# Value weights multiplied in pairs: one 512-column product over two weight slots, keys and values in another order

## The reference, cut to what matters

```
def shared_kv(x, g, w_kv):
    kv = rmsnorm(x, g) @ w_kv
    k, v = jnp.split(kv, 2, axis=-1)
...
def memory_cross_attention(u, mem_n, w_q, w_kv, w_o):
    q = (u @ w_q).reshape(b, t, MEM_HEADS, MEM_HEADDIM)
    k, v = jnp.split(mem_n @ w_kv, 2, axis=-1)
    ...
    p = jax.nn.softmax(logits, axis=-1).astype(v.dtype)
    o = jnp.einsum('bhtm,bmhd->bthd', p, v).reshape(b, t, D_MODEL)
    return o @ w_o
```

## Time and profile before

| | |
|---|---|
| median of three runs | 933.07 us (932.87 to 933.37) |
| the profiled execution | 933.03 us, span 931.2 us |
| TensorE busy | 917.2 us, 98% of the span |
| VectorE busy | 620.1 us, 67% |
| ScalarE busy | 497.9 us, 53% |
| DMA | 163.31 MB, mean 175 GB/s |

### The profile page before, as it was taken

The page is one execution under the profiler, slowest core; times in us unless marked ns, Lnnn a source line. Parts: engine busy times, 40 slices in busy tenths (PEclk is TensorE's granted clock), DMA queues, the critical chain, the costliest instruction groups (busy, mean ns, idle before and its releaser), DMA issues.

```text
span 931.2 us, 14494 instructions
## 1 busy us (share of the span) xinstructions
PE 917.2 (98%) x5972; PEld 822.5 (88%) x5972; DVE 620.1 (67%) x750; ACT 497.9 (53%) x721; POOL 56.0 (6%) x68
## 2 busy tenths in 40 slices
PE   8999999999999999999999999999999899999997
PEld 7999998878899898888888999987998798888885
DVE  6888466895765687777744764775755748777543
ACT  6565467664654564444434753665744645444333
POOL 1000003460000000000000220000000000000000
PEclk9999999999999999999999999999999899999999
DMA  9865454225562475555555696433642455555551
GB/s 276 274 187 184 142 155 132 94 99 181 181 226 92 136 229 193 196 192 181 182 195 203 212 285 214 136 137 120 215 164 91 157 172 189 182 180 183 200 204 45
DMA packets 121210, 163.31 MB, mean 175 GB/s; under 512 B 4093, under 2 KB 106933, under 8 KB 121158
## 3 DMA queue, kind: packets, MB, share of 16 engines
q1 hardware_dynamic: 117830, 151.47, 49.9%
q0 software_dynamic: 3328, 11.10, 3.8%
HBM read 161.49 MB, written 1.07 MB: 175 GB/s over the span
## 4 chain that ended last, share of the span: by engine, by line
PE 94%; DVE 3%; ACT 2%; issue 1%; DVEq 0%; ACTq 0%
PE bank L465 25%; PE bank L533 16%; PE bank L548 9%; PE bank L476 8%; PE bank L481 8%; PE bank L487 8%; PE bank L539 8%; PE bank L647 2%; PE bank L853 1%; PE bank L824 1%; PE bank L742 1%; PE bank L959 1%; PE bank L659 0%; PE bank L949 0%; DVE w_lo L1336 0%
## 5 line engine op out<-in xcount | busy, mean ns | idle before, releaser
L1336 DVE TENSOR_TENSOR w_lo<-w_raw,w_hi 128x2048 fp32r<-128x2048 f32 x135 | 308.8, 2292 | 134.9 <-ACT w_hi L991 134.4
L991 ACT ACTIVATE w_hi<-w_raw 128x2048 fp32r<-128x2048 f32 x135 | 257.4, 1913 | 201.3 <-DMA w_raw<-in_ffn_w_gu_dram 96.3
L533 PE MATMUL bank<-actT,w_hi 128*128 128x512 f32 x640 | 152.9, 391 | 0.1
L533 PEld LDWEIGHTS bank<-actT,w_hi 128*128 128x128 f32 x640 | 117.6, 188 | 23.1 <-issue 0.2
L539 PEld LDWEIGHTS bank<-actT,w_lo 128*128 128x128 f32 x640 | 82.0, 191 | 3.1
L539 PE MATMUL bank<-actT,w_lo 128*128 128x256 f32 x640 | 83.0, 283 | 0.0
L476 PE MATMUL bank<-actT,w_hi 128*128 128x256 f32 x560 | 74.3, 285 | 0.0
L481 PE MATMUL bank<-actT,w_hi 128*128 128x256 f32 x560 | 72.9, 283 | 0.0
L487 PE MATMUL bank<-actT,w_lo 128*128 128x256 f32 x560 | 72.9, 283 | 0.0
L476 PEld LDWEIGHTS bank<-actT,w_hi 128*128 128x128 f32 x560 | 69.6, 191 | 1.3 <-issue 0.8
L481 PEld LDWEIGHTS bank<-actT,w_hi 128*128 128x128 f32 x560 | 69.7, 192 | 0.0
(11 more groups left out here) (239 smaller groups left out, 1354.4 us busy)
## 6 DMA issues: line engine op xcount, KB each, us to landing
w_raw<-in_ffn_w_gu_dram SPq DMA_DIRECT2D x44, 1024.0 KB, 5.1
w_raw<-in_ffn_w_down_dram SPq DMA_DIRECT2D x22, 1024.0 KB, 4.9
w_raw<-in_ssm_w_in_dram SPq DMA_DIRECT2D x20, 1024.0 KB, 5.4
w_raw<-in_mem_w_kv_dram SPq DMA_DIRECT2D x16, 1024.0 KB, 5.5
w_raw<-in_ssm_w_out_dram SPq DMA_DIRECT2D x8, 1024.0 KB, 5.0
w_raw<-in_mem_w_q_dram SPq DMA_DIRECT2D x8, 1024.0 KB, 6.4
w_raw<-in_mem_w_o_dram SPq DMA_DIRECT2D x8, 1024.0 KB, 5.0
w_raw<-in_w_kv_dram SPq DMA_DIRECT2D x8, 1024.0 KB, 5.5
```

The lines of the kernel that those rows point to most:

```text
L533: pe.matmul(bank[:, b + c, :], hi[:, slot, cols], actT[:, k].rearrange("p e n -> p (e n)"), start=k == 0, stop=False, skip_group_check=True)
L991: act.activation(hi[:, u % SLOTS, :], raw[:, u % SLOTS, :], ACT.Copy).then_inc(w_hi_done, 1)
L1336: dve.tensor_tensor(lo[:, s, :], raw[:, s, :], hi[:, s, :].bitcast(F32), ALU.subtract).then_inc(w_lo_done, 1)
```

## The change

`MOBA_UNITS` is put into the order mk0, mk1, mv0, mv1, mk2, mk3, mv2, mv3. Eight V units (`v0` 2 and 3, `v1` 2 and 3, all of `mv`) are multiplied in pairs by a new function `wide`: one matmul has the stationary token tile as before, but streams 512 columns, 256 out of the slot of the first unit and 256 out of that of the second. Where the first unit of a pair stood, TensorE now makes token tile 0 for both units, where the second stood, tile 1 for both; each bank holds one token tile and is copied out in one piece. The first of the two waits for `w_hi` and `w_lo` of both units. Both slots are released together, after tile 1 (`w_used` by 2); the copy of tile 0 waits for a new semaphore, `wide_mm`. A half for `turn` is now four of the eight blocks of input channels. The outputs of head pairs 0 to 3 need both units of the first `mv` pair, those of 4 to 7 both of the second.

```diff
@@ -58,7 +58,8 @@
 C_ID, C_TRI, C_CAUS, C_HOT, C_END = 0, P, P + S, 2 * P + S, 2 * P + 2 * S
 
 
-MOBA_UNITS = [(name, i) for i in range(D // TC) for name in ("mk", "mv")]
+MOBA_UNITS = [(name, i + k) for i in range(0, D // TC, 2) for name in ("mk", "mv") for k in range(2)]
+WIDE = [("v0", 2), ("v0", 3), ("v1", 2), ("v1", 3), *[("mv", i) for i in range(D // TC)]]
 KIND = {"xbc": "T", "z": "T", "w_out": "M", "k0": "T", "v0": "V", "q0": "T", "wo0": "M", "gu0": "T", "down0": "M",
         "mq": "T", "mk": "T", "mv": "V", "mo": "M", "k1": "T", "v1": "V", "q1": "T", "wo1": "M", "gu1": "T", "down1": "M"}
 
@@ -103,6 +104,7 @@
 
 BANKED = [("params", 0)] + [n for n in NAME_OF if KIND[n[0]] != "M" and not (n[0] == "gu1" and n[1] < HEAD)]
 V_OF = {n: v for v, n in enumerate(BANKED)}
+WIDES = [n for n in BANKED if n in WIDE]
 FREED = []
 _n = {"act": 0, "dve": 0}
 for _name, _i in BANKED:
@@ -313,6 +315,7 @@
         head_turned, head_hi, head_lo = sem("head_turned"), sem("head_hi"), sem("head_lo")
         gate_ready, h_ready = sem("gate_ready"), sem("h_ready")
         stored = sem("stored")
+        wide_mm = sem("wide_mm")
 
         class Own:
 
@@ -557,8 +560,35 @@
                 pe.wait_ge(w_lo_done, u + 1)
                 return v_products(u % SLOTS, b, act_hi, lo, halves, last=True)
 
+            def wide(name, i, act_hi, act_lo, parts=range(2)):
+                t, u, v = i % 2, U[(name, i - i % 2)], V_OF[(name, i)]
+                s, s1 = u % SLOTS, (u + 1) % SLOTS
+                assert U[(name, i - t + 1)] == u + 1
+                for part in parts:
+                    if part == 0:
+                        e, n = FREED[v - 2]
+                        pe.wait_ge(t_out[e], n)
+                    for act, w in ((act_hi, hi), (act_lo, hi), (act_hi, lo)):
+                        if part == 0 and t == 0 and act is act_hi:
+                            pe.wait_ge(w_lo_done if w is lo else w_hi_done, u + 2)
+                        for k in range(part * KD // 2, (part + 1) * KD // 2):
+                            one = w[:, s, k * TC:(k + 1) * TC]
+                            both = bass.AP(one.tensor, one.offset, [list(one.ap[0]), [(s1 - s) * UNIT, 2], [1, TC]])
+                            ins = pe.matmul(bank[:, v % 2, :], act[:, k, t * P:(t + 1) * P], both,
+                                            start=act is act_hi and w is hi and k == 0, stop=w is lo and k == KD - 1,
+                                            skip_group_check=True)
+                    if part:
+                        if t:
+                            ins.then_inc(w_used, 2)
+                        else:
+                            ins.then_inc(wide_mm, 1)
+
             def banked(name, i, act_hi, act_lo, free=None):
 
+                if (name, i) in WIDE:
+                    wide(name, i, act_hi, act_lo)
+                    return
                 u, v = U[(name, i)], V_OF[(name, i)]
                 e, n = free or FREED[v - 2]
                 pe.wait_ge(t_out[e], n)
@@ -574,6 +604,9 @@
 
             def fill_half(name, i, half):
 
+                if (name, i) in WIDE:
+                    wide(name, i, memT_hi, memT_lo, [half])
+                    return
                 u, v = U[(name, i)], V_OF[(name, i)]
                 if half == 0:
                     e, n = FREED[v - 2]
@@ -961,7 +994,7 @@
                 if s > BLAG:
                     p = s - BLAG - 1
                     pe.wait_ge(b_probT, p + 1)
-                    e, n = FREED[V_OF[("mv", p // 2)]]
+                    e, n = FREED[V_OF[("mv", p // 4 * 2 + 1)]]
                     pe.wait_ge(t_out[e], n)
                     if p >= 2:
                         pe.wait_ge(b_lo, p - 1)
@@ -1044,13 +1077,18 @@
             def copy_out(name, i):
 
                 u, v = U[(name, i)], V_OF[(name, i)]
-                act.wait_ge(w_used, u + 1)
+                if (name, i) in WIDE and i % 2 == 0:
+                    act.wait_ge(wide_mm, sum(n[1] % 2 == 0 for n in WIDES[:WIDES.index((name, i)) + 1]))
+                else:
+                    act.wait_ge(w_used, u + 1)
                 src = tiles(v % 2)
                 dst = {"mq": mqT, "mk": mkT, "mv": mV, "k0": memK, "k1": memK, "v0": memV, "v1": memV, "q0": qT, "q1": qT}[name]
                 if name == "mq":
 
                     src = bank[:, v % 2, :].rearrange("p (c n) -> p c n", n=P)
                     dst = reversed_last(mqT[:].rearrange("p k (t n) -> p (k t) n", n=P)[:, 4 * i:4 * i + 4, :])
+                elif (name, i) in WIDE:
+                    src, dst = bank[:, v % 2, :], dst[:, i % 2, i // 2 * 2 * TC:(i // 2 + 1) * 2 * TC]
                 elif KIND[name] == "V":
                     dst = dst[:, :, i * TC:(i + 1) * TC]
                 else:
```

## The result

The changed kernel takes 935.57 us, median of nine runs (935.28 to 936.48), against 933.07 us of nine runs of the kernel before (932.63 to 933.82): a ratio of 1.003, 95% interval 1.0022 to 1.0038. It is slower by 0.3%, 2.5 us.

The account below looks back on a forecast made before the run. TensorE's stream was taken as the bound (busy 98% of the span, 94% of the last chain). From 933.03 us, products -1.23, waits +2.85 and +1.15, the rest 0, gave +2.77: 935.8 us, range 934.6 to 937.2.

Parts of the forecast that it names:

- The sum: Whole kernel: products -1.23 us, waits +2.85 and +1.15, the rest 0, so +2.77 us on 933.03.
- The wait in step 1: Self-attention, first wide `mv` pair: TensorE waits 1.70 us for `w_hi` of entry 3, then 1.15 us for its `w_lo`.
- The wait in step 5: Self-attention, mv2 with mv3: TensorE waits 0.08 us for `w_hi` of entry 7, then 1.07 us for its `w_lo`.
- The price of a product: Wide products: 226.8 ns each against 239.6 ns for two narrow ones, saving 0.61 us per pair of units.
- that rival: Wide products: a split operand makes each dearer than 226.8 ns; at 239.6 ns the kernel takes 937.0 us; chance 0.06.
- The `v` pairs: `v0` and `v1` pairs, before `q0` and `q1`: gain 0, lost waiting for VectorE; rival keeping -1.2 us, 934.6, chance 0.07.
- the 0.46 us at `ntmp`: Norm after `w_out`: three shorter halves save 0.46 us, which turns into waiting for VectorE's last half tile of `ntmp`.
- The paired release of slots: Before `q0` and `q1`: later loads covered, by 1.5 us at worst; rival late load, 937 to 939 us, chance 0.05.
- The rival with the weights in time: Steps 1 and 5: weights ready, `mv` gain alone 931.8 us, chance 0.07; with full 2.45 us, 930.6, chance 0.03.
- The clock: Step 1: rival that TensorE's clock falls during the 2.85 us wait, costing 3.6 us over 16 products, 939.4; chance 0.02.

Follow-up runs that it names:

- early preparation: Changed kernel with, in steps 0 and 4, ScalarE's `w_hi` of entry s+3 before copying out entry s+1 and VectorE's `w_lo` before the scores: 931.69 us, ratio 0.9985.
- the `v` pairs alone: Kernel before with only `v0` 2, 3 and `v1` 2, 3 multiplied wide, slots released in pairs, self-attention and order as before: 933.26 us, ratio 1.0001.

## Why the prediction was right, point by point

- **The sum and its size.** 935.8 us forecast, 935.57 measured, inside 934.6 to 937.2; the waits of 2.85 and 1.15 us, less 1.23, gave +2.77, and the stretch of the self-attention grew by 2.93. The 0.16 us between them are a saving of 1.13 us instead of 1.23 on the `mv` pairs, and waits of 4.06 us instead of 4.00, by the difference of the changed kernel's stretch to the one with early preparation. That the medians differ by 2.50 us only was not forecast. Between the two profiled executions, 0.4 us are given back at 740, where the one of before had its clock down; how much of that is in the medians no run shows. So the mechanism was right, and that the median came within 0.3 us of the forecast is in part luck.
- **The wait in step 1** had been worked out from one row of ScalarE and one of VectorE, their starts and lengths, and the program's order: 1.70 + 1.15 us against 1.72 + 1.06 us seen. Without these waits, in the kernel with early preparation, the same step is 2.86 us shorter (9.38 and 6.52 us from scores to scores).
- **The wait in step 5**: 0.08 + 1.07 against 8.42 to 9.34 us from scores to scores, 0.92 us net of the 0.3 us that the unit got shorter: 1.2 us (9.34 and 8.14 us with and without the wait).
- **The price of a product.** In the changed kernel's trace four of the new products take 588.99 - 588.08 = 0.91 us from start to start, 227 ns each. Beside it stand the 0.29 and 0.27 us that steps without a wait got shorter; 0.307 was forecast. A split moving operand costs nothing that shows: that rival is out. The Trainium skill (TensorE: Matmul & The Clock Gate, "Wait — 56ns, not 53.3ns?") has a fixed part of about 2.5 ns for each product. By that figure, as an estimate, a unit of 24 merged products would have got 0.06 us shorter; the trace has 0.27 to 0.29, and the trace decides.

```profile
588.08 1.07 PE L578 MATMUL bank<-w_lo,actT 128*128 128x512 f32 x4
...
588.99 1.98 PE L578 MATMUL bank<-w_hi,actT 128*128 128x512 f32 x8
```

- **The `v` pairs: 0.** For the `v1` pair 61.68 before, 61.67 after, 61.68 with the `v` pairs alone. The step of the argument, that VectorE's `ntmp` and its turned half end when TensorE wants them, is shown for the second by moving it away. That the 0.46 us at `ntmp` are lost for the same reason is read from the rows, it was not taken away by an experiment.
- **The paired release of slots** was covered, as said: in the changed kernel ScalarE stands 2.71 us for the load of `q0` unit 2, and the first score product starts at 274.76, 25.00 us after the first product of the `v0` pair (249.76); before it was 25.01 us (273.85 and 248.84).
- **The rival with the weights in time** was not what happened, but its price was right: with the weights made in time by an edit of the two helpers, 931.69 us, where 931.8 was written.
- **The clock.** Given 2%, it did not come in step 1 of the changed kernel's profiled run (granted clock 1.00 from 575 to 585). The single wait of 2.55 us shows that the danger was there; its price, 3.6 us for 16 products at half the rate, was too high, for the fall that was seen cost 1.61 us.

The rows of ScalarE at the start of the memory attention, on which the point on the paired release rests, in the changed kernel:

```profile
268.30 1.91 ACT L1024 ACTIVATE w_hi<-w_raw 128x2048 fp32r<-128x2048 f32 x1 [2.71 <-DMA w_raw<-in_mem_w_q_dram]
...
270.11 0.58 ACT L1096 ACTIVATE qT<-bank 128x512 f32<-128x512 f32 x1
```

`q0` unit 0 is copied out at 270.69, 4 us before 274.76, where the scores want it.

## What to carry to other kernels

A merged instruction that reads two prefetched buffers needs both at its start and frees both at its end: look one buffer further down each helper's program order before counting what the merge saves, for the wait is there even where the loads land early. Of two waits in a row, taking away the first gave nothing here, since the second ended at a time of its own; taking away the second gave its own length (2.1 us of 4.06 at the two places). And where a stretch is filled with independent work while a norm is worked out, making the filling shorter gave nothing until the last thing of the norm was moved.

## What the runs showed of the hardware

- **A wait of TensorE can bring its clock down, and the same wait does not always do it.** In the profiled runs, 1.72 and 1.06 us with 1.8 us of products between them left the granted clock at 1.00, its upper level (2.4 GHz); 2.55 us in one piece was followed by 4 us at 0.57 of it, most of that at the lower one (1.2 GHz). It is not shown that one piece is what matters: at the norm before `gu1` two waits, of 2.02 and 0.69 us with the transposes between them, are the same in all ten traces, and the clock fell there in six of them and not in the other four.
- **A fall of the clock can be free.** At this norm it fell in the profiled runs of the kernels before and after, and not in that of the kernel with early preparation. There, TensorE stood and waited for `w_hi` instead. After, at 741:747 clock 0.72 and only 0.17 us of wait behind it:

```profile
741.00:747.00 6.00, 6.00 (x38) 6.00 (x39) 4.45 (x12) 2.46 (x8) 0.53 (x1) 0.72 0.44 156
...
738.87 1.32 PE L680 MATMUL bank<-const,ntmp 128*128 128x128 f32 x8 [2.02 <-DVE ntmp L1432]
...
748.53 2.17 PE L551 MATMUL bank<-w_hi,actT 128*128 128x256 f32 x16 [0.17 <-ACT w_hi L1024]
...
754.04 1.03 PE L680 MATMUL bank<-const,ntmp 128*128 128x128 f32 x8
```

  With early preparation, clock 1.00 in that place and a wait of 1.64 us:

```profile
738.00:744.00 6.00, 4.65 (x39) 4.45 (x38) 4.42 (x12) 3.69 (x8) 0.53 (x1) 1.00 0.41 135
...
744.29 2.17 PE L552 MATMUL bank<-w_hi,actT 128*128 128x256 f32 x16 [1.64 <-ACT w_hi L1025]
```

  The slower products used time that would have been idle: from the transposes of the first token tile to those of the second it is 15.17 us after (738.87 to 754.04) and 15.18 with early preparation. It is free only as long as it fits into that wait. In the kernel before the clock was down sooner and for longer (0.82 at 732:738, 0.61 at 738:744), no wait on `w_hi` was left, and the same distance is 15.55 us:

```profile
735.06 1.68 PE L647 MATMUL bank<-const,ntmp 128*128 128x128 f32 x8 [2.02 <-DVE ntmp L1394]
...
750.61 1.03 PE L647 MATMUL bank<-const,ntmp 128*128 128x128 f32 x8
```

  That is the 0.4 us that the changed kernel's span gives back here.
- **Profiled executions differ before the changed code is reached.** The first 24 matmuls, which only keep TensorE busy, take 4.56 us in the profiled run of before and 5.28 us in that of after, and the scores of step 0 start anywhere from 573.98 to 575.30 us in the ten traces. For effects of 0.1 to 0.3% the distance between two marks that enclose the change told more than spans: where nothing between the marks had been changed it repeated to 0.04 us.
